# One stream of expert rows across steps, and another order of a head's rows on VectorE, in a two-layer hybrid attention and PEER kernel

## The reference

```python
sh1, sc1, g1, sh2, sc2, g2 = modulation(cond, p['w_ada'], p['b_ada'])
outs, state = token_mixer(x * (1 + sc1) + sh1, p)
x = layer_norm(ALPHA * x + g1 * merge_groups(outs, p['out_norm_g'], p['w_out']), p['ln1_g'], p['ln1_b'])
x = layer_norm(ALPHA * x + g2 * peer_ffn(x * (1 + sc2) + sh2, p), p['ln2_g'], p['ln2_b'])
```

```python
fv, fi = lax.top_k(cand, PEER_TOPK)
eid = jnp.take_along_axis(cid, fi, -1)
gate = jax.nn.softmax(fv, -1)
act = jax.nn.gelu(jnp.einsum('thkd,td->thk', p['peer_u'][eid], xb, preferred_element_type=jnp.float32))
return jnp.einsum('thk,thkd->td', (gate * act).astype(xb.dtype), p['peer_v'][eid])
```

## Time and profile before

| | |
|---|---|
| time before | 5282.86 us, median of 3 runs (5281.63 to 5284.09) |
| the profiled execution | 5288.38 us, of which its span is 5286.6 us |
| mean granted TensorE clock | 0.757 |
| busy: PE, DVE, POOL, ACT | 3032.0, 3434.8, 2815.9, 633.4 us |
| DMA | 1690.09 MB, mean 320 GB/s; POOL's queue of gathers 1353.39 MB, 67.7% of the 16 engines' time |

### The profile page before, as it was taken

One profiled execution on the slowest core, in us unless ns is written; L12 is line 12 of the kernel. 1 busy time (PEld: TensorE's weight loads), 2 busy tenths in 40 slices (PEclk: granted clock), 3 DMA queues, 4 the chain that ended last, 5 costly groups with the idle time before them and its releaser, 6 DMA issues. The chain is left out here.

```text
span 5286.6 us, 34528 instructions
## 1 busy us (share of the span) xinstructions
PE 3032.0 (57%) x9560; PEld 1575.4 (30%) x9560; DVE 3434.8 (65%) x6877; ACT 633.4 (12%) x1577; POOL 2815.9 (53%) x2837
## 2 busy tenths in 40 slices
PE   7638766366356546547554676645554663565354
PEld 1423344134133223311232333423332331332111
DVE  1255467677776866773568555667686677769775
ACT  0101121120121111000110001111111201211000
POOL 1116645366466646644654564445664664665675
PEclk8768868678678767778777786777776886787676
DMA  8447778789899988989896878769898998998998
GB/s 337 159 184 247 250 281 339 292 334 390 309 346 356 352 328 329 393 313 368 325 361 259 307 242 305 286 259 348 343 377 316 337 391 305 339 358 345 355 404 322
DMA packets 439839, 1690.09 MB, mean 320 GB/s; under 512 B 53120, under 2 KB 66496, under 8 KB 427568
## 3 DMA queue, kind: packets, MB, share of 16 engines
q0 software_dynamic: 370528, 1353.39, 67.7%
q1 hardware_dynamic: 69120, 334.49, 16.4%
HBM read 1660.02 MB, written 33.95 MB: 320 GB/s over the span
## 5 line engine op out<-in xcount | busy, mean ns | idle before, releaser
L571 PE MATMUL ps<-ring,diag 128*128 128x512 f32 x1456 | 875.8, 747 | 844.8 <-ACT diag L545 748.7
L502 POOL DMA_INDIRECT ring<-in_peer_u,eid_s x728 | 785.8, 1079 | 596.0 <-DVE dots L603 360.0
L502 POOL DMA_INDIRECT ring<-in_peer_v,eid_s x728 | 737.8, 1013 | 487.1 <-PE ps L571 217.7
L502 POOL DMA_INDIRECT W<-in_peer_v,eid_s x552 | 570.4, 1033 | 349.7 <-issue 125.9
L571 PE MATMUL ps<-W,diag 128*128 128x512 f32 x1104 | 618.8, 698 | 234.2 <-DMA W<-in_peer_v,eid_s 164.6
L603 DVE CUSTOM_DVE_ANT_0 ring<-ring,ps 128x1024 f32<-128x1024 f32 x552 | 658.4, 1217 | 142.4 <-DMA ring<-in_peer_u,eid_s 139.5
L603 DVE CUSTOM_DVE_ANT_0 W<-W,ps 128x1024 f32<-128x1024 f32 x552 | 655.6, 1217 | 102.0 <-DMA W<-in_peer_u,eid_s 100.7
L571 PEld LDWEIGHTS ps<-ring,diag 128*128 128x128 f32 x1456 | 320.7, 235 | 1296.8 <-issue 1126.0
L502 POOL DMA_INDIRECT W<-in_peer_u,eid_s x552 | 540.5, 979 | 292.6 <-DVE dots L603 130.1
L613 DVE SCALAR_TENSOR_TENSOR acc<-ring,wsel,acc 128x1024 f32<-128x1024 f32 x364 | 474.2, 1303 | 99.1 <-DMA ring<-in_peer_v,eid_s 69.5
L613 DVE SCALAR_TENSOR_TENSOR acc<-W,wsel,acc 128x1024 f32<-128x1024 f32 x276 | 354.8, 1286 | 50.0 <-DMA W<-in_peer_v,eid_s 24.7
(11 more groups left out here) (212 smaller groups left out, 3311.5 us busy)
## 6 DMA issues: line engine op xcount, KB each, us to landing
W<-in_w_q SPq DMA_DIRECT2D x40, 2048.0 KB
W<-in_w_ada SPq DMA_DIRECT2D x24, 2048.0 KB
W<-in_w_out SPq DMA_DIRECT2D x10, 4096.0 KB, 30.5
W<-in_w_in SPq DMA_DIRECT2D x16, 2048.0 KB, 10.1
ring<-in_peer_u,eid_s POOLq DMA_INDIRECT x728, 6.7
ring<-in_peer_v,eid_s POOLq DMA_INDIRECT x728, 6.3
toep<-mod_rows SPq DMA_DIRECT2D x20, 512.0 KB, 8.7
aux<-mod_rows SPq DMA_DIRECT2D x19, 512.0 KB, 5.7
```

The lines of the kernel that those rows point to most:

```text
L502: pool.indirect_dma_start(slot(E, r), None, a["peer_u"] if kind == "u" else a["peer_v"], bass.IndirectOffsetOnAxis(ap=eid_s[:, h % 4, k:k ...
L571: last = pe.matmul(acc_ps[:, c * 512:(c + 1) * 512], diag[:, (E.by_pe[r] - 1) % DIAGS, :], slot(E, r)[:, c * 512:(c + 1) * 512], start=Fal ...
```

## The change

The `Experts` objects go. There is one `Stream` with the rows of all ten jobs (layer and block) in one order: 16 u rows of a job ahead, then u and v by turns, and at the end of a job the 16 v rows that are left. A step has a `Slice` of that stream: `n` rows, whether it is deep, how many jobs are routed by then, and how many rows beyond its end may be gathered (`ahead`, 8, or 16 where the step that follows is deep as well). POOL issues the gather of a row as soon as the row that last had its slot lies within the slice and is used, so the gathers for the next step's first 8 or 16 rows are issued in the step before and are in flight, or landed, over the barrier; the semaphores on which they are counted are no longer cleared. The indices are read where SP puts them (`eid_e`, double-buffered like the gates), without the copies.

The sizes: input steps of latent blocks take 40 rows (32 before), the first attention step of a layer 80 (128), full attention steps 256 (256), the second modulation 72 (64), the context's input step 40 (32), its attention step 160 (160), the step with experts alone 272 (256). The first attention step stops 16 rows short of its block's end, so that a block's last 16 rows and its last sum fall into the step after (the context's of layer 1 excepted, which ends with the step). `last_sum` becomes a generator: it does one operation after each row of VectorE instead of all in a piece (`yield`), and POOL's power follows the gather of the row `RSTD_AT` further on. The clearing of `acc`, and the two products that zeroed the PSUM accumulator, go: the first row of each starts it instead (`start=opens`, `tensor_scalar_mul`).

In attention `HEAD_MID` becomes two thirds of a head's share (6 of 9) instead of a half (4), and VectorE does the last third between `finish(i)` and `negate_max(i + 2)`.

```diff
+class Stream:
+    JOB = PH * HEAD_ROWS
+    def __init__(self, jobs):
+        one = [("u", h, k) for h in range(PH) for k in range(TOPK)]
+        two = [("v", h, k) for h in range(PH) for k in range(TOPK)]
+        order = one[:LEAD]
+        for i in range(len(two)):
+            order += one[LEAD + i:LEAD + i + 1] + two[i:i + 1]
+        assert len(order) == self.JOB
+        self.rows = [(j,) + row for j in range(jobs) for row in order]
...
+    def place(self):
+        self.slot, self.landed, self.prev = [], [], []
+        user, count = [-1] * DEEP, [0] * DEEP
+        for i, S in enumerate(self.slices):
+            from_shallow = i == 0 or not self.slices[i - 1].deep
+            for r in range(S.start, S.end):
+                wide = S.deep and not (from_shallow and r < S.start + RING)
+                at = min(range(DEEP if wide else RING), key=lambda n: (user[n], n))
+                self.slot.append(at)
+                self.prev.append(user[at])
+                user[at] = r
+                count[at] += 16
+                self.landed.append(count[at])
...
+    def __init__(self, stream, n, deep, routed, ahead):
+        self.stream, self.deep = stream, deep
+        self.start = stream.slices[-1].end if stream.slices else 0
+        self.end = self.start + n
+        self.n = n
+        self.limit = min(self.end + ahead, stream.JOB * routed)
...
-        def last_sum(dve, tiles):
+        def last_sum(dve, j, tiles):
             link = chain(dve, end_chain)
-            link(dve.tensor_tensor(acc[:, :], acc[:, :], acc_ps, ALU.add))
+            r = stream.last(j)
+            dve.wait_ge(used_dve, by_dve[r])
+            dve.wait_ge(used_pe, by_pe[r])
+            ins = dve.tensor_tensor(acc[:, :], acc[:, :], acc_ps, ALU.add)
+            ins.then_inc(acc_free, 1)
+            dve.wait_ge(acc_free, j + 1)
+            yield
+            yield
             dve.wait_ge(end_in, 64)
             link(dve.tensor_tensor(acc[:, :], acc[:, :], tiles[1], ALU.mult))
+            yield
             link(dve.scalar_tensor_tensor(acc[:, :], tiles[0], ALPHA, acc[:, :], ALU.mult, ALU.add))
-            layer_norm(link, dve, acc[:, :], tiles[2], tiles[3], tiles[0], st12e, mve, vee[:, :], rstde[:, :],
-                       end_var, end_rstd, 1).then_inc(end_done, 1)
+            yield
+            link(dve.bn_stats(st12e[:, 0, :], acc[:, 0:512]))
+            link(dve.bn_stats(st12e[:, 1, :], acc[:, 512:1024]))
+            link(dve.bn_aggr(mve[:, :], st12e[:, :, :].rearrange("p a n -> p (a n)")))
+            dve.tensor_scalar_add(vee[:, :], mve[:, 1:2], EPS).then_inc(end_var, 1)
+            for _ in range(8):
+                yield
+            dve.wait_ge(end_rstd, 1)
+            link(dve.tensor_scalar(acc[:, :], acc[:, :], mve[:, 0:1], rstde[:, :], ALU.subtract, ALU.mult))
+            yield
+            link(dve.tensor_tensor(acc[:, :], acc[:, :], tiles[2], ALU.mult))
+            yield
+            dve.tensor_tensor(tiles[0], acc[:, :], tiles[3], ALU.add).then_inc(end_done, 1)
...
-        def experts_sync_ended(sp, E):
-            if E is not None and E.ended is not None:
+        def experts_sync_ended(sp, S):
+            if S is not None and S.ended is not None and not S.at_end:
                 sp.wait_ge(end_done, 1)
-                sp.dma_start(of_block(x_dram, E.ended), ended_tiles[0]).then_inc(end_stored, 16)
-        def experts_gpsimd_ended(pool, E):
-            if E is not None and E.ended is not None:
-                last_sum_rstd(pool)
-        def experts_vector_ended(dve, E):
-            if E is not None and E.begin:
-                if E.ended is not None:
-                    last_sum(dve, ended_tiles)
-                    dve.wait_ge(end_done, 1)
-                dve.memset(acc[:, :], 0.0).then_inc(acc_zero, 1)
-        def experts_sync_end(sp, E):
-            if E is None:
+                sp.dma_start(of_block(x_dram, JOBS[S.ended][1]), ended_tiles[0]).then_inc(end_stored, 16)
...
+            def rows(share):
+                t = S.target(share)
+                while pool_at[0] < S.limit and stream.prev[pool_at[0]] < t:
+                    r = pool_at[0]
+                    j, kind, h, k = rows_of[r]
+                    if r == stream.first(j):
+                        pool.wait_ge(ids_in, 16 * (j + 1))
+                    p = stream.prev[r]
+                    if p >= 0:
+                        _, q, _, qk = rows_of[p]
+                        if on_pe(q, qk):
+                            pool.wait_ge(used_pe, by_pe[p])
                         else:
-                            pool.wait_ge(used_dve, E.by_dve[r - E.slots])
+                            pool.wait_ge(used_dve, by_dve[p])
                     pool.indirect_dma_start(
-                        slot(E, r), None, a["peer_u"] if kind == "u" else a["peer_v"],
-                        bass.IndirectOffsetOnAxis(ap=eid_s[:, h % 4, k:k + 1], axis=0)).then_inc(gath[r % E.slots], 16)
-                    at[0] += 1
-            gather_until(E.slots)
-            def rows(share):
-                gather_until(E.target(share) + E.slots)
+                        row_tile(r), None, a["peer_u"] if kind == "u" else a["peer_v"],
+                        bass.IndirectOffsetOnAxis(ap=eid_e[:, j % 2, h * TOPK + k:h * TOPK + k + 1], axis=0)).then_inc(gath[stream.slot[r]], 16)
+                    pool_at[0] += 1
...
-            HEAD_MID = HEAD_SHARE // 2
+            HEAD_MID = HEAD_SHARE * 2 // 3
...
                         if i + 1 < NH:
                             negate_max(i + 1)
-                        if i == 1:
-                            experts_vector_ended(dve, E)
-                        rows(i * HEAD_SHARE)
                         rows(i * HEAD_SHARE + HEAD_MID)
                         finish(i)
+                        rows((i + 1) * HEAD_SHARE)
                     rows(A_END)
...
+        TAIL_ROWS = TOPK
+        IN_ROWS = 40
+        FIRST_ROWS = Stream.JOB - NLAT * IN_ROWS - TAIL_ROWS
+        MOD_ROWS, CTX_ROWS = TAIL_ROWS + 56, 160
+        def take(n, deep, routed, ahead=RING):
+            return Slice(stream, n, deep, routed, ahead)
+        parts = []
+        for L in range(DEPTH):
+            j = L * NBLK
+            parts += [take(IN_ROWS, False, j + 1) for _ in range(NLAT)]
+            parts.append(take(FIRST_ROWS, True, j + 1, DEEP))
+            parts += [take(Stream.JOB, True, j + b, DEEP) for b in range(2, LAST)]
+            if L + 1 < DEPTH:
+                parts.append(take(Stream.JOB, True, j + LAST))
+                parts.append(take(MOD_ROWS, False, j + NBLK))
+                parts.append(take(IN_ROWS, False, j + NBLK))
+                parts.append(take(Stream.JOB + TAIL_ROWS - MOD_ROWS - IN_ROWS, True, j + NBLK))
+            else:
+                parts.append(take(Stream.JOB, True, j + LAST, DEEP))
+                parts.append(take(Stream.JOB + TAIL_ROWS, True, j + NBLK))
...
+            for b in range(1, NBLK):
+                step_input(L, b, False, b == 1, next(part))
+            step_attend_route(L, 1, False, True, next(part), shares=4)
             for b in range(2, NBLK):
-                step_input(L, b, False, False, Experts(L, 0, b - 1, 1, landings=landings))
-            step_attend_route(L, 1, False, True, Experts(L, 0, NLAT, PH - NLAT, slots=DEEP, landings=landings))
-            step_attend_route(L, 2, False, False, Experts(L, 1, 0, PH, begin=True, ended=0, slots=DEEP, landings=landings))
-            for b in range(2, LAST):
-                step_attend_route(L, b + 1, False, False, Experts(L, b, 0, PH, begin=True, ended=b - 1, slots=DEEP, landings=landings))
+                step_attend_route(L, b, False, False, next(part))
```

More of the change, by code:

```diff
@@ L62 @@
 DIAGS = 4
+LEAD = TOPK
 SHARES = {
@@ L70 @@
 }
[L74 to L83, removed]
 def on_pe(kind, k):
     return kind == "v" and k % BY_PE == 0
[L90 to L101, removed]
+class Stream:
[8 more added lines that the diff above has]
+        self.rows = [(j,) + row for j in range(jobs) for row in order]
         self.by_dve, self.by_pe = [], []
         d = p = 0
-        for kind, _, k in self.order:
+        for _, kind, _, k in self.rows:
             if on_pe(kind, k):
@@ L111, in __init__, with first, last, next_u @@
             self.by_pe.append(p)
[L113 to L117, removed]
+        self.pe_through = [p for (_, kind, _, k), p in zip(self.rows, self.by_pe) if kind == "v" and k == TOPK - 1]
+        self.slices = []
+    def first(self, j):
+        return j * self.JOB
+    def last(self, j):
+        return (j + 1) * self.JOB - 1
+    def next_u(self, r):
+        while r < len(self.rows) and self.rows[r][1] != "u":
+            r += 1
+        return r
+    def place(self):
[11 more added lines that the diff above has]
+                self.landed.append(count[at])
+class Slice:
+    def __init__(self, stream, n, deep, routed, ahead):
[4 more added lines that the diff above has]
```

(30 more changed lines are left out.)

271 lines of the change are left out of this document (136 added, 135 removed).

## The result

The changed kernel takes 5422.70 us (median of 4 runs, 5411.97 to 5433.29) against 5283.48 us: the ratio is 1.0261, with a 95% interval of 1.0238 to 1.0283. It is slower by 2.6%, where 5038 us was forecast. The profiled execution took 5424.51 us, its span is 5422.7 us.

What follows compares the result with a forecast made beforehand. Full attention steps were taken as bound by transfers for some 380 us, then by VectorE for 77. The terms -174 - 124 + 60 + 12 - 16 - 3 = -245 gave 5043, or 5038 us for the median; range 4900 to 5165.

Steps and rivals of the forecast that it cites:

- the barrier waits for what is in flight: Rival, chance 0.08: POOL's drain at 18 barriers holds until gathers land, costing 266 us; 5304 us in all.
- the term of the input steps: Nine input steps, 40 rows instead of 32: +9 in two first ones, +6 in seven others, together +60 us.
- So thirteen end at 563.2 + 16.1: Steady input step: thirteen POOL gathers behind the rotary embedding, ending at 563.2, finish at 579.3; behind the +6 us.
- The price of a row is the slope between the two: (454.7 - 305.7)/128 = 1.16 us: First attention steps: 48 rows fewer save 56 us; with the band's wait -62 each, -124 us for two.
- 10 us only: Heads of full attention steps: room for transfers when rows fill the waits for scores; 8 us taken a step.
- The 21 us for 16 gathers moved into the last part: Full attention steps: 16 next-step gathers move into VectorE's last 77 us, so the transfer-bound part loses 21 us.
- the 2.65 us waits for scores gone from the list: Sign of being right: VectorE's 2.65 us waits for scores in attention heads disappear.
- signs of being wrong: Full steps of 440 us or more at share above 0.95, drains of microseconds, value-product waits beyond 14.7, input steps past 84.
- The lower ceiling: Rival, chance 0.05: transfers in mixed steps are limited to 357 GB/s, full steps gain 14 us instead of 29; 5128 us.
- The experts-alone step: Step with experts alone: 256 gathers still bind it, -3 us.
- the +12 of the forecast: Second modulation, 72 rows instead of 64: +12 us, from 8 more gathers, last rows needn't land, and later weight pieces.
- its -16: Context's attention step of layer 1: rows landed at its start and u and v by turns bring -16 us.

Runs made afterwards that it cites:

- e1: The changed kernel with block ends and barriers of steps with expert rows made of semaphores alone, without POOL's drain: 5297.42 us, 1.0019 times the kernel before.
- e5: The changed kernel with 32 rows (16 u, then 16 v) in latent input steps, 112 in first attention steps, and barriers without POOL's drain: 5203.82 us, 0.9834.
- e6: The kernel before with only VectorE's new order in a head (two thirds of the rows ahead of the output's scaling, a third behind): 5134.69 us, 0.9704.

## Why the prediction was wrong

**The barrier.** The rival "the barrier waits for what is in flight" was the mechanism; it got a chance of 0.08. The step that failed is its evidence, "that takes 41 to 47 ns now, but no gather was ever in flight there": it is the wrong drain of two. Its price, 266 us from the transfer time of all gathers ahead, lies near the eleven barriers with 8 gathers ahead (10.6 us each there, 10.1 measured) and is too high for the seven with 16 (21.3, and 11.7 measured), where more of them have landed by VectorE's end; 193 us are exposed, and 125 come back when the drain goes (e1). Its 5304 us were too low, since the term of the input steps was off besides.

**Input steps.** "So thirteen end at 563.2 + 16.1" took the end of the embedding as fixed. It moved by 12 us with the rows ahead of it, and behind VectorE's last row the drain held on: +26 to +28 where +6 stood, seven times, and +25 and +23 where +9 stood. Taken over nine steps this term alone is 182 us off.

**First attention steps.** "The price of a row is the slope between the two: (454.7 - 305.7)/128 = 1.16 us" failed. Without the drain, 80 rows take 281 us (e1), 112 take 294 (e5): 0.4 us a row; e6, with 128 rows and nothing in flight, takes 289. Where rows go, VectorE waits for the step's own work instead. Its waits in this step of the changed kernel, and in e6's with 128 rows (the product with the values first, then a copy of ScalarE, and in the changed kernel the scores, 13.1 us, where e6 has 8.7):

```profile
DVE aux L1399 <- PE ps L1231: 30.6, 9, 5.2
...
DVE big L1446 <- ACT W L1329: 25.2, 1, 25.2
...
DVE big L1373 <- PE ps L1212: 7.3, 6, 2.7
DVE small L1378 <- PE ps L1212: 5.8, 4, 2.7
```

```profile
DVE aux L1350 <- PE ps L1178: 13.7, 9, 4.7
...
DVE big L1399 <- ACT W L1277: 7.8, 1, 7.8
```

So of 48 rows that cost 0.4 us each there, 32 were moved to input steps, where a row costs 1.6; the other 16 went to the step after. And about 10 us of each first step's end are the drain.

**Full steps: two terms, both mis-sized.** The order in a head was capped at "10 us only" by the busy share of 0.95; it brings 14 to 21 a step, 18.6 on average (e6). The share was a poor measure of room: in e6 the same stretch runs at 405 GB/s where it ran at 357, so in rate there was room for 13%. The 21 us for 16 gathers moved into the last part bring next to nothing: e1's full steps are 1.5 us shorter than e6's on average. The gathers do move (e1: share 0.91 there), and the heads begin 10 us earlier, but they get no shorter, 155.0 us at a share of 0.93 against 153.3 at 1.02, and the part between heads and end gets longer, 184.0 us against 178.9. That the engines' own chain binds there once the waits for scores are gone is my reading; no run parts it from the transfers. With the drain added, 444 us on average instead of 426. The sign "the 2.65 us waits for scores gone from the list" came true in full steps; in the first attention step 13.1 us of them are left. Three of the signs of being wrong came too: drains of microseconds, input steps past 84, and waits for the product with the values of 19.1 us in a full step and 30.6 in a first one.

**The lower ceiling.** The case of 357 GB/s is refuted by e6's heads. The rule cited for it, about 358 GB/s in the Trainium skill's "DMA: Bandwidth & Descriptors", section "Where 436 GB/s comes from", isn't a limit here: 405 GB/s over 153 us. The Trainium skill's "HBM Reference", section "Specifications (TRN2)", says that a core streaming alone measures well above that share, and the row agrees.

**What held.** The experts-alone step and the rest of the list are small; the modulation's +20 is +13 at VectorE's end, near the +12 of the forecast, and the drain; that the parts of those 12 were right is not shown. The context's attention step met its -16 in this profile, but other runs of nearly the same code have it at 322 to 328 us, so that isn't settled. Nor is which engine sets the 1.6 us of a row in an input step.

## What to carry to other kernels

Before issuing transfers ahead over a barrier, look for every instruction that stands between the last issue and the next step, on the issuing engine above all, and ask what it waits for when something is in flight. A slope between two steps prices work only while the same thing binds both; moving work out of a step that its own chain binds gains little, and costs where the chain is longer for it. And test the parts of a change one by one: here a gain of 3% stood hidden behind a loss of nearly twice that.

## What was not expected of the hardware

A drain of POOL holds at least until the gathers that POOL has issued have landed: in the input steps medians of 8.1 us before and 11.2 after, in the second case with no other engine at work, with the last packet 2 us or more ahead of the drain's end, and without that wait in the kernel whose barriers have no drain (e1). It isn't landing alone: in the context's attention step of layer 1 the drain takes 5.1 us with the last gather's packet 35 us behind it, and what it waits for there stays open. And a mean DMA busy share of 0.95 at 357 GB/s wasn't a full queue: the same twelve heads, freed of VectorE's waits, ran at 1.02 and 405 GB/s.
